# Key pages, conv states and constants in another order on the load queue of a decoder layer

## The reference, cut to what matters

```python
z = x @ w_in                              # q | k | v | B | C | h
q, k, v, gb, gc, h = jnp.split(z, SPLITS, axis=-1)
att = attend(q, k, v)                     # samples: block means of all cached keys, top 3 blocks, softmax
conv_y, conv_buf_new = causal_dwconv(gc * h, conv_buf, w_conv)
x1 = layer_norm(ALPHA * x + concat(att, gb * conv_y) @ w_out, ln1_g, ln1_b)
up, ffn_buf_new = causal_dwconv(x1 @ w_up, ffn_buf, w_fconv)
a, g = jnp.split(up, 2, axis=-1)
y = layer_norm(ALPHA * x1 + (silu(a) * g) @ w_down, ln2_g, ln2_b)
```

## Time and profile before

| | us |
|---|---|
| median of 3 runs | 447.43 |
| lowest and highest run | 447.05, 448.56 |
| the profiled execution, its own time | 448.32 |
| its span in the trace | 446.5 |
| TensorE busy | 416.1 (93%) |
| VectorE busy | 296.0 (66%) |
| ScalarE busy | 181.6 (41%) |
| GpSimd busy | 104.4 (23%) |
| bytes moved, mean rate | 124.85 MB, 280 GB/s |

### The profile page before, as it was taken

The page is one execution under the profiler, slowest core; times in us unless marked ns, Lnnn a source line. Parts: engine busy times, 40 slices in busy tenths (PEclk is TensorE's granted clock), DMA queues, the critical chain, the costliest instruction groups (busy, mean ns, idle before and its releaser), DMA issues.

```text
span 446.5 us, 8259 instructions
## 1 busy us (share of the span) xinstructions
PE 416.1 (93%) x2911; PEld 341.0 (76%) x2911; DVE 296.0 (66%) x383; ACT 181.6 (41%) x694; POOL 104.4 (23%) x133
## 2 busy tenths in 40 slices
PE   4999999999999998999798989999999999999990
PEld 4588887876866774664364369999999999999990
DVE  0496999999799976944351264766666877534536
ACT  1476568653377334011110043455554456224201
POOL 1003033995255231100000436211222221000002
PEclk9999999999999999999999999999999999999997
DMA  8999999999999999999999953566666685968002
GB/s 294 385 329 386 385 388 379 370 357 390 398 386 372 351 393 387 386 386 386 386 377 386 304 166 111 159 178 189 189 182 170 166 215 155 234 174 212 24 1 97
DMA packets 109515, 124.85 MB, mean 280 GB/s; under 512 B 5775, under 2 KB 66920, under 8 KB 109466
## 3 DMA queue, kind: packets, MB, share of 16 engines
q1 hardware_dynamic: 101138, 107.55, 72.5%
q10 hardware_dynamic: 8336, 16.78, 10.5%
HBM read 121.90 MB, written 2.61 MB: 279 GB/s over the span
## 4 chain that ended last, share of the span: by engine, by line
PE 55%; DVE 18%; SPq 11%; issue 6%; DMA 5%; POOL 2%; ACT 1%; DVEq 0%; POOLq 0%; ACTq 0%
PE ps L1815 11%; PE ps L1816 11%; PE ps L1817 11%; SPq L354 8%; DVE qk L930 5%; DVE T L940 5%; PE ps L1432 4%; PE ps L1627 4%; PE ps L1708 3%; PE ps L1603 3%; PE ps L1629 3%; PE ps L1372 3%; DMA wring<-in_cache_v 2%; DMA KV<-in_cache_k 2%; POOL x1l L605 1%
## 5 line engine op out<-in xcount | busy, mean ns | idle before, releaser
L1177 DVE TENSOR_TENSOR wlo<-KV,whi 128x2048 fp32r<-128x2048 f32 (+1 forms) x24 | 61.8, 2576 | 57.1 <-ACT whi L832 29.1
L1432 PE MATMUL ps<-xT,wring 128*128 128x264 f32 x384 | 89.6, 389 | 0.0
L1432 PEld LDWEIGHTS ps<-xT,wring 128*128 128x128 f32 x384 | 71.9, 191 | 13.4 <-issue 1.7
L1815 PE MATMUL ps<-x1h,whi 128*128 128x264 f32 x256 | 73.8, 288 | 0.2
L930 DVE TENSOR_TENSOR qk<-KV,qk 128x1536 f32<-128x1536 f32 (+1 forms) x32 | 67.8, 2122 | 9.2 <-DMA KV<-in_cache_k 5.5
L1817 PE MATMUL ps<-x1h,wlo 128*128 128x264 f32 x256 | 72.7, 284 | 0.0
L1816 PE MATMUL ps<-x1l,whi 128*128 128x264 f32 x256 | 72.7, 284 | 0.0
L662 ACT ACTIVATE qk<-qk 128x64 f32<-128x64 f32 x216 | 51.8, 244 | 28.5 <-POOL qk L553 21.1
L940 DVE TENSOR_REDUCE T<-qk 128x24 f32<-128x1536 f32 (+1 forms) x32 | 58.4, 1827 | 0.0
L1815 PE MATMUL ps<-fh,whi 128*128 128x264 f32 x176 | 50.4, 286 | 0.1
L1816 PE MATMUL ps<-fl,whi 128*128 128x264 f32 x176 | 50.0, 284 | 0.0
(11 more groups left out here) (218 smaller groups left out, 578.9 us busy)
## 6 DMA issues: line engine op xcount, KB each, us to landing
KV<-in_cache_k SPq DMA_DIRECT2D x128, 256.0 KB, 7.3
KV<-in_w_ffn_up SPq DMA_DIRECT2D x32, 512.0 KB, 5.1
KV<-in_cache_v SPq DMA_DIRECT2D x60, 256.0 KB, 8.5
wring<-in_cache_v SPq DMA_DIRECT2D x56, 256.0 KB, 7.5
KV<-in_w_ffn_down SPq DMA_DIRECT2D x8, 1408.0 KB, 7.0
wring<-in_w_in ACTq DMA_DIRECT2D x5, 2048.0 KB, 15.1
zbuf<-in_cache_v SPq DMA_DIRECT2D x12, 256.0 KB, 6.0
zbuf<-in_w_ffn_up SPq DMA_DIRECT2D x3, 1024.0 KB, 11.5
```

The costliest lines, as they stand in the source:

```text
L1177: nc.vector.tensor_tensor(wlo[s][:, 0:n], w2[s][:, 0:n], whi[s][:, 0:n], ALU.subtract).then_inc(s_lo, 1)
L1432: ins = nc.tensor.matmul(ps[:, z_bank(n), 0:R], tile[k], xT[:, k, :], start=k == 0, stop=k == KT - 1)
L1815: nc.tensor.matmul(out, wh[k], xh[k], start=k == 0, stop=False)
```

## The change

It is in SyncE's list alone. The loads of slots (1, 0) and (1, 1) now stand ahead of the four loads of the conv states and taps; these follow, and then slots (1, 2) and (1, 3). The eight constants, which stood ahead of all of these, are split: four behind slot (2, 0) and four behind slot (2, 1).

```diff
--- before.py
+++ after.py
@@ -362,14 +362,6 @@
             ids = page_ids(1)
             up_tiles = slice(0, 2 * FT)
             mixer_tiles = slice(2 * FT, 48)
-            sp.dma_start(stack[up_tiles, 0:STATE_ROWS, :],
-                         state_ffn_conv[0].rearrange("b k (n d) -> n (b k) d", d=P)).then_inc(s_stack, 16)
-            sp.dma_start(stack[up_tiles, STATE_ROWS:STACK, :],
-                         w_ffn_conv[0].rearrange("k (n d) -> n k d", d=P)).then_inc(s_stack, 16)
-            sp.dma_start(stack[mixer_tiles, 0:STATE_ROWS, :],
-                         state_conv[0].rearrange("b k (n d) -> n (b k) d", d=P)).then_inc(s_stack, 16)
-            sp.dma_start(stack[mixer_tiles, STATE_ROWS:STACK, :],
-                         w_conv[0].rearrange("k (n d) -> n k d", d=P)).then_inc(s_stack, 16)
             consts = ((dist, c_dist), (alibi, c_bias.rearrange("p g h -> p (g h)")), (slope, c_slope), (diag, c_diag),
                       (headmask, c_head), (tri, c_tri),
                       (lnr[0:8, :], ln1_g.rearrange("o (k p) -> (o k) p", p=P)),
@@ -419,13 +411,24 @@
                 first = a * FF + QUAD * P
                 sp.dma_start(pairs[a], wup[:, :, first:first + 2 * P]).then_inc(s_eu[4 + a], 16)
 
-            load_consts(0, 8)
-            for s in range(SLOTS):
-                load_keys(1, s, ids)
+            load_keys(1, 0, ids)
+            load_keys(1, 1, ids)
+            sp.dma_start(stack[up_tiles, 0:STATE_ROWS, :],
+                         state_ffn_conv[0].rearrange("b k (n d) -> n (b k) d", d=P)).then_inc(s_stack, 16)
+            sp.dma_start(stack[up_tiles, STATE_ROWS:STACK, :],
+                         w_ffn_conv[0].rearrange("k (n d) -> n k d", d=P)).then_inc(s_stack, 16)
+            sp.dma_start(stack[mixer_tiles, 0:STATE_ROWS, :],
+                         state_conv[0].rearrange("b k (n d) -> n (b k) d", d=P)).then_inc(s_stack, 16)
+            sp.dma_start(stack[mixer_tiles, STATE_ROWS:STACK, :],
+                         w_conv[0].rearrange("k (n d) -> n k d", d=P)).then_inc(s_stack, 16)
+            load_keys(1, 2, ids)
+            load_keys(1, 3, ids)
             for b in range(2, 5):
                 ids = page_ids(b)
                 for s in range(SLOTS):
                     load_keys(b, s, ids)
+                    if b == 2 and s < 2:
+                        load_consts(4 * s, 4 * s + 4)
             ids, ids_v = page_ids(5), page_ids(0)
             load_keys(5, 0, ids)
             load_quad(0)
```

## The result

The changed kernel is slower: 449.85 us (median of 8 runs, 449.33 to 451.17) against 447.55 us (8 runs of the kernel before on the same chip, 447.05 to 448.6). The ratio is 1.0047 with a 95% interval of 1.0032 to 1.0062. That is outside the forecast range of 445.0 to 449.2 us. The profiled execution took 449.55 us with a span of 447.8 us, against 448.32 and 446.5 us before.

The account below looks back on a forecast made before the run. The prediction took the DMA byte stream to bound the kernel up to 246.79 us. TensorE's delay at the constants, less waits shed, left -0.5 us against the 447.43 us median, hence 446.9 us; range 445.0 to 449.2 us.

Parts of the forecast that it names:

- part 2: Conv states behind the first key slots: down at 36.3 us (at worst 38.2), so no TensorE wait at 37.12.
- part 3: Constants behind (2, 0) and (2, 1): down at 54.7 us (52.5 to 56.4), TensorE standing 1.8 us.
- Part 1: Key pages ahead of small loads: VectorE's 3.53 us wait before 36.90 us goes, its product starts at 33.4.
- Where the two meet: TensorE and VectorE, 70 to 103 us: waits of 1.06, 0.41, 0.86 us shrink or go; TensorE leaves 0.5 us early.
- The stream: DMA bytes: 0.75 us late at 88 us, regained at 140 to 154 us, last value slot 0.5 us early.
- (b): Rival, chance 0.18: constants at 56.4 us, or states after 37.12; TensorE stands 3.5 us; +1.7, 449.1 us.
- (a): Rival, chance 0.25: constants down when TensorE comes, which sheds 2.3 us of waits; about -2.0, 445.4 us.

Follow-up runs that it names:

- e2: Kernel before with only the constants moved behind slots (2, 0) and (2, 1), states still ahead of the key pages; ratio 1.0063.
- e8: Kernel before with the constants moved late and TensorE's turn of the layer norm rows moved late too; ratio 0.9985.
- e12: Same kernel as e8, measured again against the kernel before; ratio 0.9987.
- e1: Changed kernel with states still behind the first two key slots, but all eight constants directly behind the states; ratio 1.0023.
- e3: Changed kernel with five idle products on TensorE ahead of its wait for the conv states; ratio 1.0049.
- e9: Changed kernel with only the turn of the layer norm rows moved behind the ninth tile and first head scores; ratio 1.0002.
- e13: Changed kernel with the 44 state and tap rows loaded in parts of 32 and 12; ratio 1.0061.
- e14: Changed kernel with the 44 state and tap rows loaded in parts of 33 and 11; ratio 1.0042.
- e5: Changed kernel with only TensorE's turn of the conv states moved behind the fifth tile; ratio 1.0085.
- e6: Changed kernel with twelve idle products on TensorE ahead of its wait for the conv states; ratio 1.0087.
- e4: Changed kernel with both turns, of conv states and of layer norm rows, moved later on TensorE; ratio 0.9984.
- e11: Same kernel as e4, measured again against the kernel before; ratio 1.0000.

## Why the prediction was wrong, step by step

Two landing times of the forecast failed, that of the states in part 2 and that of the constants in part 3. The experiments put the loss on the second.

**Part 1 held.** The 3.53 us of VectorE went, and the next reduction followed at once (33.51 us for 33.4 forecast).

**Part 2 failed.** The states were forecast at 36.3 us with 38.2 as the upper end; TensorE had them at 38.93. The step that failed is "the short rows now run with no w_in beside them", taken as a reason for a better rate. The stretch 32 to 40 us had 266 GB/s in the change, a loss of 8 x (1 - 266/387) = 2.5 us for the states alone. Beside w_in the states and the constants together cost 1.7 us (300 and 362 GB/s); in e2 the states alone went down there, at 292 GB/s from 22 to 28 us and 369 from 28 to 32, again 1.7 us, and e8 and e12 had 384 and 381 GB/s from 32 to 40. So the effect has the other sign, and is worth some 0.8 us. ScalarE's queue moved nothing from 32 to 40 us in the change. The likely reading is that large rows of a second queue fill what short rows leave unused; no run moved w_in to test it by itself. So TensorE's wait was 1.80 us for a forecast of 0.

**A term was missing, and its cost was mostly hidden.** Neither the forecast nor a rival priced TensorE's clock. In four kernels (the change, e1, e3, e9) a wait of 0.90 to 1.83 us at 38 to 39 us was followed by 3.4 us at half clock, which is 1.7 us, and the waits of 3.70 and 3.85 us came with 6.8 us at half clock, of which 6.3 lay behind the wait. Waits of 2.31 and 2.08 us at the same place (e13, e14) had none behind them. The trace of before has no such wait early on, and 1.06 us at 70.10 was not followed by a fall, which made it easy to leave out. Twelve fillers show the term, 14.51 us for 16.19, and also that the change paid next to nothing for it: with full clock TensorE had the constants at 57.10 us and the last slot at 248.06, for 57.24 and 248.11. Where nothing later hides the fall, as in e2, e5 and e13, it adds to the loss.

**Part 3 failed, and it is the step that cost.** The constants were forecast at 54.7 us, at most 56.4, with TensorE standing 1.8 us; TensorE had them at 57.24, and at 57.10, 57.33, 57.69 and 57.77 in e6, e3, e14 and e13. (With part 2's upper end of 38.2 the step's own sum gives 56.6, not 56.4.) TensorE's lateness there came to 4.37 us: 1.80 of the first wait, 1.7 of the clock, 0.81 of the second wait, with under 0.1 us left over. That is how it was spent, but the constants set its length. Part 3 counted on from the states' 36.3 us, so the states' slow stretch went into it unseen; from 38.9 us the same sum gives 57.3. That is not the whole reason, though: in e2 the states were in time, 32 to 40 us ran at 384 GB/s, and the constants came at 56.68 all the same, against some 55.5 expected for it. The slow stretch is then worth about 0.6 us of the 2.5, and why the rest was late is open. That the wait for the constants is the cost is shown by e9, where only their turn was moved and the loss was gone (1.0002), beside e5, where only the states' turn was moved and it grew (1.0085).

**"Where the two meet" held as a mechanism.** The waits of 1.06, 0.41 and 0.86 us vanished as said, 2.33 us in all. With the right lateness the step gives the right answer: 4.37 - 2.33 = 2.04 us late at the transposes of the head scores, and 2.03 was measured. It holds in the experiments too, to some tenths. e1: 3.36 - 2.33 = 1.03, measured 0.92. e14: 4.82 - 2.33 = 2.49, measured 2.46. e9 has the loads of e4 and turns the layer norm rows at 60.46 us, e4 at 57.15, 3.31 earlier; it sheds e4's waits of 1.08, 0.59 and 0.86 us but for 0.16, which leaves 0.94; measured 124.01 - 123.31 = 0.70. e2 is the worst: 3.81 us late at its turn and 3.0 more by the half clock, less 2.33, gives 4.5; measured 3.94.

**"The stream" had the right two places.** The halves were forecast 0.75 us late and were 3.1; the stream was empty for 2.9 us and not 0.8. It got back 1.6 us from 140 to 154 us, the whole of what it lacked there, as both forecast and rival (b) said. Hence +1.32 at the last slot. A lateness at the transposes of 0.6 to 0.9 us (e9, e1) leaves that slot within 0.14 us of the kernel before; 2.0 leaves 1.3, and 3.9 leaves 3.7 to 4.1. What is more than the stream's slack goes to the end about one to one.

**The rivals.** (b) is what happened, the constants coming later than its 56.4 us and, by the door named in its last sentence, the states after 37.12. The halves were 3.1 us late for its 2.5 and the last slot 1.3 for its 1.7; its time of 449.1 was 0.75 us short of the median. (a), faster by 2.0 us, has no support: the orders in which nothing waits end at 0.9984 to 1.0000, that is 0 to 0.7 us. VectorE's wait of 3.53 us was thus worth next to nothing in any order tried.

This account explains 1.3 us, the difference of the two profiled spans; the medians differ by 2.3. The profiled execution of before lay 0.8 us above its median, that of the change 0.3 us below, which makes up the rest. That it is scatter was not tested.

## What to carry to other kernels

Before a small load is put behind large ones, look at which engine uses it first, and forecast its landing from a time at which the same bytes were down in a trace, not from the full rate. If other work can stand ahead of the wait, move the use in the same edit as the load. A slow clock behind a wait costs only what no later wait would have taken anyway. Short rows went down faster here while the second queue had large rows to send, 1.7 us lost for 2.5, though the orders that used it (e8, e12) were no faster in all than those that did not (e4, e11). Two waits in a row on one engine are one problem: test them as a square (neither, each alone, both), since mending the first alone can be worse than the change itself.

## What the runs showed of the hardware

A TensorE wait of 0.90 us (e3), in an engine otherwise busy all the time, was followed by 3.4 us at half clock, as were those of 1.31, 1.80 and 1.83 us, and the fall began 2.0 to 2.4 us after the wait had ended. The waits of 3.70 and 3.85 us had 6.8 us at half clock, which began within them, at 56.2 and 56.5 us. But the waits of 2.31 and 2.08 us at 39 us in e13 and e14 were not followed by a fall, nor was e14's of 2.62 us at 57.69, while e13's of 2.59 us at 57.77 was, by 3.4 us from 59.0 us on. The change also fell for 3.4 us at 218.4 us, behind a wait of 1.85 us for a value slot; the kernel before waits 1.83 us at the same place and does not fall. The wait of 1.06 us at 70.10 us in the earlier trace rows, and one of 1.08 us at 69.78 in e4, were not followed by a fall either. The length of the wait does not tell them apart; what does stays open.

An issue of one small DMA held SyncE for 3.91 us right behind another with short rows; its neighbours took 0.32 to 0.42 us. The same issue took 1.34 us in the kernel before and 3.67 in e4. And in the kernel with twelve fillers, 24 passes and their weight loads at 37 us, a wait of 1.54 us for issue stood at 274 us, far away in the program. No other kernel of the study has it; it was seen in one profile and its cause was not tested.
